# A ring of four pairs of raw weights instead of eight, filled pair by pair

## What is computed

```python
for i in range(DEPTH):
    hn = rmsnorm(x, norm_g[i])
    proj = hn @ w_in            # 2048 x 8192 (da), x 4608 (sw), x 8208 (ml)
    o = mixer(proj)             # attention or mLSTM, times silu of the gate part
    x = x + o @ w_out           # 2048 x 2048
return rmsnorm(x, final_g)
```

## Time and profile before

| | us |
|---|---|
| median of 3 runs | 1813.99 (1813.31 to 1813.99) |
| span of the profiled execution | 1813.6 |
| PE busy | 1790.8 (99%) |
| DVE busy | 1067.0 (59%) |
| ACT busy | 873.3 (48%) |
| share of the 16 DMA engines in use by the load queue | 58.9% |
| HBM read | 310.10 MB |

### The profile page before, as it was taken

How to read it: one execution, slowest core, us unless ns; L and a number is a source line. 1 busy time by engine, 2 the same in 40 slices (tenths; PEclk the granted TensorE clock), 3 DMA queues, 4 the chain that set the end, 5 groups by cost and what they waited for, 6 DMA issues and landing times.

```text
span 1813.6 us, 23603 instructions
## 1 busy us (share of the span) xinstructions
PE 1790.8 (99%) x8331; PEld 1478.9 (82%) x8331; DVE 1067.0 (59%) x1712; ACT 873.3 (48%) x1347; POOL 38.9 (2%) x102
## 2 busy tenths in 40 slices
PE   6999999999999999999999999999999999999998
PEld 5888888888887887788888888888888888888886
DVE  4766665655656665655545454545556666666555
ACT  5454544444545455545444444444554545454443
POOL 0000000000000000000000000000000000000000
PEclk8999999999999999999999999999999999999999
DMA  7655454555554434446888689965555555555462
GB/s 236 198 162 188 161 187 162 183 172 194 177 192 146 140 118 137 141 161 179 155 142 205 167 171 172 206 180 187 185 186 171 179 184 163 188 159 188 161 221 102
DMA packets 165790, 313.09 MB, mean 173 GB/s; under 512 B 5878, under 2 KB 22332, under 8 KB 165596
## 3 DMA queue, kind: packets, MB, share of 16 engines
q1 hardware_dynamic: 165676, 312.08, 58.9%
q0 software_dynamic: 48, 0.13, 0.2%
HBM read 310.10 MB, written 2.10 MB: 172 GB/s over the span
## 4 chain that ended last, share of the span: by engine, by line
PE 97%; DVE 1%; DMA 1%; ACT 0%; issue 0%; POOL 0%; SPq 0%; POOLq 0%; DVEq 0%; ACTq 0%
PE acc L808 29%; PE acc L810 29%; PE acc L809 29%; PE tp L779 4%; DMA raw<-in_da_w_in_dram 1%; PE sc L884 1%; PE sc L835 1%; PE sc L883 1%; PE sc L870 0%; PE sc L871 0%; PE sc L834 0%; PE sc L817 0%; PE sc L819 0%; PE sc L818 0%; DVE w_lo L1481 0%; PE sc L869 0%
## 5 line engine op out<-in xcount | busy, mean ns | idle before, releaser
L1481 DVE TENSOR_TENSOR w_lo<-raw,w_hi 128x1024 fp32r<-128x1024 f32 x584 | 709.1, 1223 | 527.6 <-ACT w_hi L752 527.2
L752 ACT ACTIVATE w_hi<-raw 128x1024 fp32r<-128x1024 f32 x584 | 614.9, 1058 | 540.2 <-PE acc L810 524.3
L808 PE MATMUL acc<-w_hi,xt_hi 128*128 128x512 f32 x1824 | 730.8, 401 | 9.9 <-DVE w_lo L1481 9.9
L810 PE MATMUL acc<-w_hi,xt_lo 128*128 128x512 f32 x1824 | 713.6, 391 | 0.0
L809 PE MATMUL acc<-w_lo,xt_hi 128*128 128x512 f32 x1824 | 712.0, 390 | 0.0
L808 PEld LDWEIGHTS acc<-w_hi,xt_hi 128*128 128x128 f32 x1824 | 343.3, 188 | 81.7 <-DVE w_lo L1481 10.5
L810 PEld LDWEIGHTS acc<-w_hi,xt_lo 128*128 128x128 f32 x1824 | 342.8, 188 | 72.7
L809 PEld LDWEIGHTS acc<-w_lo,xt_hi 128*128 128x128 f32 x1824 | 343.5, 188 | 68.3
L808 PE MATMUL acc<-w_hi,ot_hi 128*128 128x512 f32 x512 | 201.2, 393 | 0.0
L810 PE MATMUL acc<-w_hi,ot_lo 128*128 128x512 f32 x512 | 199.6, 390 | 0.0
L809 PE MATMUL acc<-w_lo,ot_hi 128*128 128x512 f32 x512 | 199.3, 389 | 0.0
(11 more groups left out here) (226 smaller groups left out, 1006.1 us busy)
## 6 DMA issues: line engine op xcount, KB each, us to landing
raw<-in_da_w_in_dram SPq DMA_DIRECT2D x128, 1024.0 KB, 5.6
raw<-in_ml_w_in_dram SPq DMA_DIRECT2D x48, 1024.0 KB, 8.2
raw<-in_sw_w_in_dram SPq DMA_DIRECT2D x36, 1024.0 KB, 5.0
raw<-in_da_w_out_dram SPq DMA_DIRECT2D x32, 1024.0 KB, 5.0
raw<-in_sw_w_out_dram SPq DMA_DIRECT2D x16, 1024.0 KB, 5.0
raw<-in_ml_w_in_dram SPq DMA_DIRECT2D x32, 512.0 KB, 7.9
raw<-in_ml_w_out_dram SPq DMA_DIRECT2D x16, 1024.0 KB, 5.1
xres<-in_x_dram SPq DMA_DIRECT2D x4, 512.0 KB, 14.3
```

Source lines behind the costliest of these rows:

```text
L752: act.activation(w_hi[:, q:q + 2, :], raw[:, 2 * p:2 * p + 2, :], ACT.Copy).then_inc(hi_ready, 1)
L808: pe.matmul(out_ap, k_hi, m_hi, start=start, stop=False)
L810: return pe.matmul(out_ap, k_lo, m_hi, start=False, stop=stop)
L1481: dve.tensor_tensor(w_lo[:, q:q + 2, :], raw[:, 2 * p:2 * p + 2, :], w_hi[:, q:q + 2, :].bitcast(F32), ALU.subtract).then_inc(lo_ready, 1)
```

## The change

`raw` becomes a ring of eight blocks (four pairs), as `w_hi` and `w_lo` are. Every load takes one pair (0.5 MB, or two DMAs of 0.25 MB in job 0 of `ml`), so there are twice as many. A load of pair q waits until DVE has finished pair q-4. ACT waits for the load at every pair, not at every second. In the opening, the loads of the first four pairs wait for nothing, x1, x2 and x3 are issued ahead of pairs 2, 4 and 6, and pairs 4 to 7 wait for DVE's pairs 0 to 3. `load_small` stays where it is in the program, behind the loads of the first job.

```diff
-        raw = sb("raw", [P, KC, JW])
+        raw = sb("raw", [P, RING, JW])
...
-                for q in range(0, len(OUT_ORDER), 2):
+                for q in range(len(OUT_ORDER)):
                     n, p = OUT_ORDER[q]
-                    s = q // 2 % 4
-                    sp.wait_ge(lo_ready, PAIRS * (OUT0[l] - 1) + q + 2)
-                    rows_of = w[P * 2 * p:P * 2 * p + 512, :].rearrange("(k p) n -> p k n", p=P)
-                    sp.dma_start(raw[:, 4 * s:4 * s + 4, :], rows_of[:, :, JW * n:JW * n + JW]).then_inc(raw_full[s], 16)
+                    s = q % LAG
+                    sp.wait_ge(lo_ready, PAIRS * OUT0[l] + q + 1 - LAG)
+                    rows_of = w[P * 2 * p:P * 2 * p + 2 * P, :].rearrange("(k p) n -> p k n", p=P)
+                    sp.dma_start(raw[:, 2 * s:2 * s + 2, :], rows_of[:, :, JW * n:JW * n + JW]).then_inc(raw_full[s], 16)
...
-                for s in range(4):
-                    if opening and s > 0:
-                        load_x(s)
-                    if not opening:
-                        sp.wait_ge(lo_ready, PAIRS * (J - 1) + 2 * s + 2)
-                    rows_of = w[512 * s:512 * s + 512, :].rearrange("(k p) n -> p k n", p=P)
+                for p in range(PAIRS):
+                    s = p % LAG
+                    if opening and p in (2, 4, 6):
+                        load_x(p // 2)
+                    if not opening or p >= LAG:
+                        sp.wait_ge(lo_ready, PAIRS * J + p + 1 - LAG)
+                    rows_of = w[P * 2 * p:P * 2 * p + 2 * P, :].rearrange("(k p) n -> p k n", p=P)
...
-                if p % 2 == 0:
-                    act.wait_ge(raw_full[p // 2], 16 * (J + 1))
-                    if w.kind == "ml" and w.phase == "iter" and j == 0:
-                        act.wait_ge(raw_half[p // 2], i * 16 + 16)
+                act.wait_ge(raw_full[p % LAG], 32 * J + 16 * (p // LAG + 1))
+                if w.kind == "ml" and w.phase == "iter" and j == 0:
+                    act.wait_ge(raw_half[p % LAG], i * 32 + 16 * (p // LAG + 1))
...
-                act.activation(w_hi[:, q:q + 2, :], raw[:, 2 * p:2 * p + 2, :], ACT.Copy).then_inc(hi_ready, 1)
+                act.activation(w_hi[:, q:q + 2, :], raw[:, q:q + 2, :], ACT.Copy).then_inc(hi_ready, 1)
```

More of the change, by code:

```diff
@@ L410, in load @@
                         for a, arrived in enumerate((raw_half, raw_full)):
-                            sp.dma_start(raw[:, 4 * s:4 * s + 4, half * a:half * a + half],
+                            sp.dma_start(raw[:, 2 * s:2 * s + 2, half * a:half * a + half],
                                          rows_of[:, :, bass.ds(col + pair_of * a, half)]).then_inc(arrived[s], 16)
                     else:
-                        sp.dma_start(raw[:, 4 * s:4 * s + 4, :], rows_of[:, :, bass.ds(col, JW)])\
+                        sp.dma_start(raw[:, 2 * s:2 * s + 2, :], rows_of[:, :, bass.ds(col, JW)])\
                           .then_inc(raw_full[s], 16)
@@ L1480, in pair @@
                 q = 2 * (p % LAG)
-                dve.tensor_tensor(w_lo[:, q:q + 2, :], raw[:, 2 * p:2 * p + 2, :], w_hi[:, q:q + 2, :].bitcast(F32),
+                dve.tensor_tensor(w_lo[:, q:q + 2, :], raw[:, q:q + 2, :], w_hi[:, q:q + 2, :].bitcast(F32),
                                   ALU.subtract).then_inc(lo_ready, 1)
```

## The result

The changed kernel takes 1819.92 us (median of 6 runs, 1818.26 to 1823.39), the kernel before 1813.97 beside it (6 runs, 1813.31 to 1814.67): ratio 1.0034, 95% interval 1.0022 to 1.0045. It is 6.0 us slower. The profiled execution is the quickest of the six: 1818.26, with a span of 1816.5.

A forecast was written before the change was run, and what follows sets the result against it. PE was taken to bound the kernel, 97% of the chain of waits, with loads setting the time only in the opening. Opening 4.6 plus `ml` 2.4 gave 7.0 on 1813.99, so 1821.0 us, range 1815 to 1833.

The forecast's parts named there:

- The steady stream: In `da`, `sw` and output projections, PE stalls only if a load takes over 14 us; the smaller ring costs nothing.
- The gain at the start: Opening: the first 0.5 MB load lands 1.3 us earlier, so PE begins pair 0 at 18.2 instead of 19.50.
- The wait for the small loads: Opening: small loads queue behind SP's wait for DVE's pair 3; DVE stands at L1061, PE ends 4.6 us late.
- T: Opening: time when all six small loads are in, forecast at 40.2 us; DVE stands at L1061 until then.
- rival C: Opening: PE idle 4.8 us before pair 5 lowers its clock, 2.6 us more: 1823.6 us; chance 0.06.
- The `ml` projection: Two DMA-saturated stretches of `ml`: loads outlast the smaller ring's store, PE falls short by 2.0 and 0.4, together 2.4 us.
- the count of 3.30 us a pair: Second `ml` stretch: load service time from landings, against PE's 2.92; the loads lose 11.5 us over 30 pairs.
- the store of 9.5: `ml`: us of late loading the four-pair ring can absorb before PE stalls; 2.0 short of the 11.5 lost.
- The base: Whole kernel: the runs' median of 1813.99 us, 0.4 above the profiled span of 1813.6, to which 7.0 was added.
- A: Not slower: small loads land within 3 to 4 us, the ring rides through `ml`; 1815 to 1816 us; chance 0.18.
- B: Saturated `ml`: each smaller piece costs 0.3 us extra, 18 us more; 1839 us, with half of it 1830; chance 0.12.
- D: Opening: first pair early and no wait for the small loads, faster by over 0.2%; chance 0.04.

The follow-up runs named there:

- Experiment 8: experiment 1 with a raw ring of two pairs and x2 and x3 ahead of the small loads: 2046.59 us (before 1815.16).
- experiment 2: The changed kernel with the raw ring back at eight pairs, still one DMA a pair: 1813.69 us (before 1814.87).
- experiment 1: The changed kernel with the six small loads issued ahead of the load of pair 4, behind no wait: 1814.43 us (before 1814.87).
- experiment 5: The kernel before, old ring and 1 MB loads, with SP waiting for DVE's pair 3 ahead of the small loads: 1821.12 us (before 1815.16).
- experiment 4: The changed kernel with the `ml` projection reading its weights from the `da` matrix, rows of 32768 bytes: 1819.78 us (before 1814.87).
- experiment 11: The changed kernel again, unedited, with its own profile: 1820.34 us (before 1814.83).
- experiment 3: The changed kernel with its four-pair ring filled by 1 MB loads (two places): 1853.23 us (before 1814.87).
- experiment 7: experiment 1 with GpSimd's load of the gate weights (2048 rows of 64 bytes) issued behind DVE's pair 1: 1808.33 us (before 1815.16).
- experiment 9: experiment 2 with GpSimd's load of the gate weights issued behind DVE's pair 1: 1810.70 us (before 1814.83).
- experiment 12: experiment 7 with the last quarter of x issued ahead of the small loads: 1809.45 us (before 1814.73).
- experiment 10: The kernel before, old ring and 1 MB loads, with the gate weights' load issued behind DVE's pair 1: 1811.22 us (before 1814.83).
- experiment 6: The changed kernel with DVE waiting at L1061 for only three small loads, for the other three at place 13: 1816.89 us (before 1815.16).

## Why the prediction was right, and where it was not

**The steady stream: right.** Loads of half the size landed in 3.8 us in `da`; 14 were allowed. ACT's three waits for a `da` load all lie in the opening. After the opening and outside `ml` no pair fell back by more than 0.25 us against the trace of before. Experiment 8 measured the loop itself.

**The gain at the start: right.** 1.3 was forecast. Against the one trace of before it was 2.4 and 1.7 in the two traces of the changed kernel and 0.8 in experiment 2, for the landing of the first load scatters by some 2 us from run to run. Over all traces with the gate weights in their old place, PE began pair 0 at 18.04 on average with loads of 0.5 MB (seven traces, 17.08 to 18.79) and at 19.55 with 1 MB (three, 18.81 to 20.34): 1.5 us. What the prediction left out is that the lead grows to pair 4, to 3.0 and 2.6 in the two traces of the changed kernel, since fewer of PE's first matmuls ran at the low clock (9 in the first trace, all 12 of pair 0 before).

**The wait for the small loads: right.** It is the cause, shown by experiments 1 and 5, and it took the place forecast: DVE at L1061, 5.6 us. The terms differ. The first was issued at 28.9, not at 30.6. The last was issued 2.4 us after the first, not 3.8: each took some 0.45 us, less than the 0.52 to 2.39 of before; the last landed after 5.4 (forecast 5.8). That puts T at 36.8, not at 40.2. By the prediction's own formula (T + 1.8 less 36.3 less 1.1) PE would be 1.2 late; it is 1.7, and 3.75 at this point in the second trace.

**The clock (rival C, given 0.06): wrong to put it aside.** It happened in both traces of the changed kernel, after 3.1 and 3.6 us without work, and made pair 5 longer by 1.4 and 2.6 us. It happened in experiments 4 and 5 too, after 3.5 and 2.6 us. In the first trace it turned 1.1 us of lateness (DVE ended pair 6 at 42.20, with PE ready just after) into 1.7, in the second 2.0 into 3.75. So the opening's 4.6 held two errors of opposite sign: the wait alone took PE from a lead of 3.0 and 2.6 at pair 4 to a lag of 1.1 and 2.0, 4.1 and 4.6 us, where 5.9 was forecast (1.3 + 4.6), and the clock added 0.6 and 1.75. How much of pair 5 runs at 1.2 GHz may be a part of the spread of the changed kernel's first six runs, 5.1 us against 1.4; but the seven of experiment 11 spread over 1.7 us and the runs of before beside them over 3.4, so the spread is no mark of the change.

**The `ml` projection: the mechanism came, the term did not.** ACT waits for loads in many places there, as forecast. Forecast for PE were 2.4 us; the traces give 0.6 to 0.8 and 1.1, experiment 1 gives none, and experiment 4 about 1. The step that failed is the count of 3.30 us a pair from the landings of 1 MB loads. In the changed kernel the load issued at 1076.5 landed at 1085.8 and the one issued at 1158.2 at 1167.6: 27 pairs in 81.8 us, 3.03 each. Against PE's 2.92 that is a deficit of 3 us, not 11.5, well within the store of 9.5. The count by bytes, 2.91, which I held as the lower bound, was nearly right.

The 3.30 could have been seen to be too high in the trace of before. Its first two steps, 4 pairs from 1062.1 to 1077.7, lay before the second stretch of rows 12: the loads that ended them were issued only at 1060.9 and 1068.5. Behind 1077.7 it was 26 pairs in 83.5 us, 3.21 each, and by that count too the store would have lasted. Between 3.21 and 2.91 stand the bytes still under way at the end: a load took 7.8 us from issue to landing at first and 18.9 at last. That this fills the gap is argued. In experiment 2, as deep but in small pieces, 22 pairs landed between 1085.4 and 1150.9, 2.98 each. Experiment 3 shows the other side: the same depth as the changed kernel in 1 MB loads costs 36 us in `ml` in its trace.

The path was not the one forecast either. PE was to stand short on `w_lo`. It had `w_lo` in store; what came late, by 0.4 and 0.5 us, was DVE's side work at L1219, which stands behind the late weight work.

**The base.** The profiled run of the changed kernel took 1.8 us more than its span (1818.26 and 1816.5), and the profiled runs of the experiments 1.7 to 2.0. I had taken 0.4 for before, from a span of 1813.6 and a median of 1813.99. The execution profiled before was thus more likely near 1815.3, one with a late first load, and the sum started from too slow an opening. As an estimate, the opening costs about 5 us against the median (6.0 less the 0.6 to 1.1 of `ml`), where the traces show 2.1 and 3.5. That the forecast of 1821.0 came within 1.1 us is thus partly luck: `ml` was 1.5 us too dear, the wait was priced too high and the clock left out, and the base was low in its favour (the same 7.0 on 1815.3 gives 1822.3).

**Rivals.** A failed on the opening, though its half on `ml` was right. B failed: experiment 2 has no `ml` wait at all. D did not come, and C came, as told above. The page "DMA: Bandwidth & Descriptors" of the Trainium skill asks for 1 MiB a DMA (section "Measured (HBM→SBUF, 128 partitions, SWDGE, issued from GpSimd)"). The loads here are issued by SP. With several of them under way, 0.5 MB was as good (experiment 2 at 1813.69 against 1814.87 for the kernel before, with an interval of the ratio that includes 1), and with room for four pairs only, 1 MB was the worse choice (experiment 3). That pieces could fail to overlap (0.01, in B) did not come either: in the opening of the changed kernel the first six loads of 0.5 MB behind the gains landed 1.3 us apart, from 14.7 to 21.2.

## What to carry to other kernels

When a ring gets shallower, its loads start to wait, and so does everything that the same queue issues behind them: look for the small, rarely noticed DMAs there before pricing the ring. A ring is deep enough when places times the consumer's time per piece exceeds the loop of issue, landing and the steps until the place is free; small pieces make that loop shorter and leave more of them under way. Price a short idle time of TensorE with the work that follows it at half clock as well, and price an opening from more than one trace. When a slow DMA is moved out of the way, look at what it will stand beside in its new place.

## What the runs showed of the hardware

One GpSimd load of 2048 rows of 64 bytes held up the first weights by 5 to 9 us: a first load of 0.5 MB landed at 7.5 to 8.0 us without it (experiments 7, 9 and 12) and at 14.7 to 16.4 with it (seven traces), one of 1 MB at 10.9 (experiment 10) and at 16.4 to 18.0 (three traces). TensorE's granted clock was low again after pauses of 3.1 and 3.6 us (the changed kernel), 2.6 (experiment 5) and 2.2 (experiment 10), and stayed full after 0.9 (experiment 6). Loads from rows of 32832 bytes kept the DMA engines at a share of 1.02 for 175 GB/s in 1078 to 1161, loads from rows of 32768 bytes at 0.61 for 182 GB/s (experiment 4); what in the addresses does it wasn't tried. It isn't the row length alone: in 968 to 1050 the kernel before loaded from the same long rows at a share of 0.69 for 193 GB/s.
